# Other rows for the mixing steps beside units 1 and 2, and another order of unit 0's decay, products and doubling, in a two-layer streaming encoder

## The chip, the cores and the metric

The kernel runs on one core of a Trainium2 chip, as one launch. The metric is the device time in microseconds (us), lower being better. A core has five engines that run their own instruction streams in order and meet at semaphores: PE (TensorE, matrix products into the accumulators, called banks), DVE (VectorE), ACT (ScalarE), POOL (GpSimd) and SP (SyncE). Sixteen DMA engines move the data; here SP's queue issues the loads of weights, and POOL's queue the gathers of table rows.

## What is computed

The reference is a trunk of two layers over 256 tokens of 1024 numbers. Each layer normalises, projects once (`h @ w_in`), and gives the columns to three branches whose outputs are joined and projected back; then a retrieval step picks 128 experts of 16384 for each token.

```
for l in range(2):
    h = rms_norm(x, norm_mix[l]);  cols = h @ w_in[l]
    y_a = diff_attention(cols_a, ...)       # 4 heads, softmax(0) - lam * softmax(1), block-causal in chunks of 64
    y_b = s5_mixer(cols_b, ...)             # 1024 complex states, diagonal scan over the tokens, then a gated unit
    y_c = rwkv7_mixer(cols_c, ...)          # 4 heads, S = S*w + (S @ -kk) b^T + v k^T, y = S r, for every token
    x = x + concat(y_a, y_b, y_c) @ w_out[l]
    x = x + peer_ffn(rms_norm(x, norm_ffn[l]), ...)

# peer_ffn for a block of 128 tokens
s = einsum(q, sub_keys); top 16 of each half; best 16 of the 256 sums, for each of 8 heads
act = gelu(einsum('thkd,td->thk', u_tab[expert], h))
out = einsum('thk,thkd->td', softmax(best) * act, v_tab[expert])
```

## The kernel before

The 256 tokens are two tiles of 128, and with two layers this makes four units, n = 0 to 3: layer n // 2, tile n % 2. A unit has a mixing part (projection, three branches, output projection), then a part that chooses experts, and then 256 table rows: for each of 128 slots one row of u and one of v, each 1024 numbers for 128 tokens (512 KB). POOL gathers them (line 618) into a ring of 16 buffers (`arena`). DVE multiplies a u row with the token and sums (lines 1833 and 1835). A v row is scaled and added up by PE, as two 128x512 products with a diagonal matrix that ACT makes (lines 2430, 2431, 1057), or in one case of three from slot 32 on by DVE (lines 1842 and 1846). A buffer is gathered anew once its user has let go of it.

The mixing and the choosing of unit n + 1 are cut into named steps, which stand between the rows of unit n. `ROWS_BY[n]` gives for each step the row before which it stands, 0 to 256, and DVE, PE and ACT all read the same table: `by_rows` and `gather` put the rows and the steps into each engine's stream. So the order is written out in full; nothing is scheduled at run time. Table 0 belongs to unit 0's rows and unit 1's steps, table 1 to unit 1's rows and unit 2's steps, table 2 to unit 2's rows and unit 3's steps. Unit 0's own steps have no rows to stand between; its order is in the functions `first`, one for each engine.

The steps, in their order: bc0 to bc4 and da0 to da5 are chunks of the projection, one load of weights (1 MB) and 3.6 us of PE or less each, through a ring of three buffers (`wring`) that SP fills again when a chunk has been multiplied. At da0 and da2 DVE turns the inputs of the state-space branch (`s5_turn`), at da3 and da4 it scans them (8 scans each), at da5, rot and sd it turns back and adds; gelu, glu, tanh, glud, gss are its gated unit. abkr is `products`, which makes the inputs al, bm, km, rp of the delta rule; mats are their products on PE (lines 2092); at masked DVE masks them and starts the inverse of a triangular 128x128 matrix per head. The inverse takes six levels k: p is the product on PE (lines 2117, 2122), c its copy on ACT (line 840) and the next level's factor on DVE (line 1238), u the update on PE (lines 2132, 2134), d its copy on ACT (lines 847, 848). The attention hangs on some of them: scores and their maxima at level 1 and 3, the softmax on ACT after levels 2 and 4, DVE's `combined` (line 1334) at d2 and d4. rhs, rhsd, sa, y, mean and so on end the delta rule, out3 and xm the mixing, fT to id4 choose the experts.

In unit 0 DVE also computes the turning factors of the state-space branch by doubling (`phase_doubling`, k from 0 to 6); the last and largest is k = 6.

Of the kernel before, what the change touches and what calls it, by code (L numbers as in the profile page):

```python
# [18 lines left out]
ALU = mybir.AluOpType  # L19
# [68 lines left out]
for _s in range(SLOTS - LEAD):  # L88
# [24 lines left out]
        "tanh": 100, "glud": 103, "gss": 104, "abkr": 108, "mats": 108, "masked": 119, "p1": 123, "c1": 125,  # L113
# [3 lines left out]
        "yd": 172, "mean": 175, "dev": 180, "var": 181, "vara": 185, "outd": 196, "out3": 196, "xm": 196, "fsq":  # L117
# [9 lines left out]
        86, "glu": 89, "tanh": 92, "glud": 92, "gss": 102, "abkr": 102, "mats": 102, "masked": 111, "p1": 116,  # L127
# [3 lines left out]
        "y": 165, "yd": 169, "mean": 169, "dev": 170, "var": 170, "vara": 170, "outd": 170, "out3": 173, "xm":  # L131
# [72 lines left out]
def build_program(nc, A, out):  # L204
    ctx = ExitStack()
    with ctx:
# [418 lines left out]
        def _(act):  # L625
# [53 lines left out]
            def mixing(n, layer, t):  # L679
# [191 lines left out]
                def first():  # L871
# [20 lines left out]
                    kk_length()  # L892
                    own(A_(small_a[:, 30:31], eps[:, 0:1], ACT.Exp))
                    decays()
                    output_map()
                    squares()
                    input_map()
                    qk_lengths()
# [1573 lines left out]
```

## Time and profile before

| | |
|---|---|
| median of three runs | 1729.08 us (1728.06 to 1729.99) |
| the profiled execution: its time, its span | 1729.59 us, 1727.8 us |
| mean granted TensorE clock, of full speed | 0.924 |
| PE busy, share of the span | 1339.9 us, 78% |
| DVE | 1390.0 us, 80% |
| POOL | 1137.9 us, 66% |
| ACT | 406.1 us, 24% |
| DMA | 640.89 MB, mean 371 GB/s; gathers 538.25 MB |

The span goes from the first to the last instruction. Busy shares are means over stages with different limits; an engine that isn't the limit of a stage costs nothing by idling there. A wait is put down to what released it last. The DMA share is a relative measure: where the queues are never empty it reads 1.03.

### The profile page before, as it was taken

How to read it: one execution, taken by the hardware profiler on the slowest of the kernel's cores; microseconds unless marked ns; L12 is line 12 of the kernel's file. 1: busy time of each engine (PE TensorE's matmuls, PEld its weight loads, DVE VectorE, ACT ScalarE, POOL GpSimd, SP SyncE). 2: the span in 40 equal slices, each digit the busy share in tenths (PEclk: the TensorE clock that was granted, in tenths of full speed). 3: DMA queues.
4: the chain of work that ended last, by engine and by line, in shares of the span. 5: the costliest groups of instructions: out<-in, count | busy, mean ns of one | idle time of the engine just before them, and what ended most of it. 6: DMA issues, size and time to landing. Idle time of an engine off the chain costs nothing. (4 is left out here: it accounts for less than half of the span.)

```text
span 1727.8 us, 17677 instructions
## 1 busy us (share of the span) xinstructions
PE 1339.9 (78%) x5322; PEld 755.4 (44%) x5322; DVE 1390.0 (80%) x3383; ACT 406.1 (24%) x977; POOL 1137.9 (66%) x1046
## 2 busy tenths in 40 slices
PE   6989689688889397867887868978888837765667
PEld 6568444255456163444454453444545412222222
DVE  7867999996779789996777898987777897687663
ACT  2442312333211221413221122313221121101000
POOL 2002776777775876477767777577777777777773
PEclk9999899999999699999999979989999969988889
DMA  7348999999999999899999999999999999999997
GB/s 236 135 158 284 398 403 362 410 382 365 408 402 399 404 393 405 313 357 355 385 393 404 403 404 407 366 375 354 387 403 402 409 410 409 410 409 410 409 409 313
DMA packets 204721, 640.89 MB, mean 371 GB/s; under 512 B 18602, under 2 KB 35860, under 8 KB 204628
## 3 DMA queue, kind: packets, MB, share of 16 engines
q0 software_dynamic: 147920, 538.25, 80.0%
q1 hardware_dynamic: 56172, 100.96, 16.2%
q8 instruction: 43, 0.70, 0.2%
q10 hardware_dynamic: 536, 0.57, 0.1%
q14 instruction: 50, 0.41, 0.1%
HBM read 638.65 MB, written 1.05 MB: 370 GB/s over the span
## 5 line engine op out<-in xcount | busy, mean ns | idle before, releaser
L618 POOL DMA_INDIRECT arena<-in_peer_u_dram,expert x512 | 562.0, 1098 | 346.1 <-issue 139.7
L618 POOL DMA_INDIRECT arena<-in_peer_v_dram,expert x512 | 566.3, 1106 | 210.2 <-issue 139.3
L2430 PE MATMUL bank<-arena,diag 128*128 128x512 f32 x768 | 433.8, 648 | 242.4 <-DMA arena<-in_peer_v_dram,expert 171.1
L1835 DVE SCALAR_TENSOR_TENSOR arena<-arena,normed 128x1024 f32<-128x1024 f32 x364 | 434.5, 1225 | 63.0 <-DMA arena<-in_peer_u_dram,expert 58.6
L2431 PE MATMUL bank<-arena,diag 128*128 128x512 f32 x768 | 416.9, 626 | 0.0
L2430 PEld LDWEIGHTS bank<-arena,diag 128*128 128x128 f32 x768 | 133.8, 199 | 453.7 <-issue 386.9
L2431 PEld LDWEIGHTS bank<-arena,diag 128*128 128x128 f32 x768 | 154.3, 201 | 200.3 <-issue 200.3
L1833 DVE SCALAR_TENSOR_TENSOR arena<-arena,bank 128x1024 f32<-128x1024 f32 x148 | 176.9, 1219 | 80.7 <-DMA arena<-in_peer_u_dram,expert 80.1
L1057 ACT ACTIVATE diag<-ident,weight 128x128 f32<-128x128 f32 x384 | 129.9, 392 | 211.5 <-DVE weight L1852 119.6
L1910 PE MATMUL bank<-h_cm,wring 128*128 128x128 f32 x1152 | 143.6, 287 | 27.8 <-DMA wring<-in_peer_w_q_dram 8.4
L1910 PEld LDWEIGHTS bank<-h_cm,wring 128*128 128x128 f32 x1152 | 141.3, 202 | 39.6 <-issue 24.5
L1846 DVE SCALAR_TENSOR_TENSOR x<-arena,weight,x 128x1024 f32<-128x1024 f32 x96 | 123.5, 1286 | 21.8 <-DMA arena<-in_peer_v_dram,expert 20.2
L1926 PE MATMUL bank<-wring,h_cm 128*128 128x512 f32 x192 | 91.6, 626 | 10.6 <-DMA wring<-in_w_in_dram 8.7
L1061 ACT ACTIVATE dots<-dots 128x16 f32<-128x16 f32 x32 | 6.9, 216 | 332.7 <-DVE arena L1835 174.6
L1926 PEld LDWEIGHTS bank<-wring,h_cm 128*128 128x128 f32 x192 | 37.5, 201 | 57.4 <-issue 41.8
L1934 PE MATMUL bank<-wring,h_cm 128*128 128x512 f32 x128 | 59.7, 613 | 2.2 <-DVE h_cm L1562 1.1
L1842 DVE SCALAR_TENSOR_TENSOR bank<-arena,weight,bank 128x1024 f32<-128x1024 f32 x30 | 38.6, 1288 | 14.2 <-DMA arena<-in_peer_v_dram,expert 13.3
L1061 ACT ACT_TABLE_LOAD x24 | 30.8, 1283 | 61.7 <-DVE arena L1835 33.1
L1791 DVE SCALAR_TENSOR_TENSOR work<-work 128x64 f32<-128x64 f32 (+1 forms) x320 | 41.1, 202 | 0.7
L1934 PEld LDWEIGHTS bank<-wring,h_cm 128*128 128x128 f32 x128 | 25.1, 199 | 31.9 <-issue 29.5
L840 ACT ACTIVATE work<-bank 128x512 f32<-128x512 f32 x24 | 14.2, 593 | 83.6 <-PE bank L2122 83.3
L2122 PEld LDWEIGHTS bank<-work 128*128 128x128 f32 x192 | 24.9, 191 | 14.4 <-issue 10.4
(445 smaller groups left out, 1534.7 us busy)
## 6 DMA issues: line engine op xcount, KB each, us to landing
wring<-in_w_in_dram SPq DMA_DIRECT2D x40, 1024.0 KB, 12.9
wring<-in_peer_w_q_dram SPq DMA_DIRECT2D x25, 1024.0 KB, 15.0
wring<-in_w_out_dram SPq DMA_DIRECT2D x16, 1024.0 KB, 8.9
arena<-in_peer_u_dram,expert POOLq DMA_INDIRECT x512, 12.8
arena<-in_peer_v_dram,expert POOLq DMA_INDIRECT x512, 13.7
arena<-in_peer_w_q_dram SPq DMA_DIRECT2D x7, 1024.0 KB, 11.5
wring<-in_w_in_dram SPq DMA_DIRECT2D x4, 512.0 KB, 13.2
x<-in_x_dram SPq DMA_DIRECT2D x2, 512.0 KB, 5.3
```

What stands on the lines that cost most here:

```text
L618: nc.gpsimd.indirect_dma_start(out=rows[g % RING], out_offset=None, in_=tables[kind], in_offset=bass.IndirectOffsetOnAxis(ap=expert[:, n % ...
L1057: A_(diag[:, p % DIAGS, :], ident[:, :], ACT.Copy, scale=weight[:, slot:slot + 1]).then_inc(s_diag, 1)
L1791: last = stt(picks[c // 8][:, c % 8, :].rearrange("p (a b) -> p a b", b=TOPK), places, float(c), ids, ALU.is_equal, ALU.mult)
L1833: ins = stt(row2, row2, 1.0, hb_psum[n], ALU.mult, ALU.mult, accum_out=dots[:, slot:slot + 1])
L1835: ins = stt(row, row, 1.0, hb, ALU.mult, ALU.mult, accum_out=dots[:, slot:slot + 1])
L1842: ins = stt(total, row2, weight[:, slot:slot + 1], so_far, ALU.mult, ALU.add)
L1846: ins = stt(x[:, t, :], row, weight[:, slot:slot + 1], x[:, t, :], ALU.mult, ALU.add)
L1910: last = mm(bank[b0 + j][:, 0:P], w[:, k, P * j:P * j + P], source[:, 4 * part + k, :], start=part == 0 and k == 0, stop=part == 1 and k == 3)
L1926: last = mm(bank[b0][:, :], h_cm[:, 4 * part + k, :], w[:, k, :], start=part == 0 and k == 0, stop=part == 1 and k == 3)
L1934: last = mm(bank[4 + half_][:, :], mixed[:, OUT_K[name] + k, :], w[:, k, 512 * half_:512 * half_ + 512], start=name == "out0" and k == 0, ...
L2430: mm(bank[6][:, :], d, row[:, 0:512], start=first, stop=end)
L2431: mm(bank[7][:, :], d, row[:, 512:1024], start=first, stop=end).then_inc(s_pe_used, 1)
```

## The change

Three things are changed. First, table 1 (rows of unit 1, steps of unit 2) from exp4 on to d6, and second, table 2 (rows of unit 2, steps of unit 3) from late_id4 to masked, give their steps other rows. The values of table 0 and table 3 stay. Of table 1, row before and row now:

| step | late_id4 | gate4 | da0 | da1 | da2 | da3 | da4 | da5 | rot | sy | sd | glu | glud | abkr | mats |
|---|---|---|---|---|---|---|---|---|---|---|---|---|---|---|---|
| before | 65 | 71 | 71 | 71 | 71 | 73 | 74 | 75 | 75 | 77 | 83 | 89 | 92 | 102 | 102 |
| now | 65 | 65 | 66 | 69 | 72 | 76 | 80 | 85 | 89 | 92 | 96 | 101 | 106 | 111 | 113 |

| step | masked | p1, c1 | u1, d1 | p2 | c2 | u2, d2 | p3 | c3 | u3, d3 | p4, c4 | u4, d4 | p5 | c5 | p6 to u6 | d6 | rhs |
|---|---|---|---|---|---|---|---|---|---|---|---|---|---|---|---|---|
| before | 111 | 116 | 118 | 124 | 126 | 126 | 136 | 136 | 139 | 144 | 144 | 147 | 149 | 153 | 154 | 156 |
| now | 121 | 124 | 127 | 131 | 132 | 133 | 138 | 139 | 141 | 145 | 146 | 149 | 150 | 154 | 155 | 156 |

Of table 2:

| step | late_id4 | da0 | da1 | da2 | da3 | da4 | da5 | rot | sy | glud | gss | abkr | mats | masked |
|---|---|---|---|---|---|---|---|---|---|---|---|---|---|---|
| before | 46 | 48 | 53 | 54 | 54 | 54 | 56 | 65 | 68 | 91 | 91 | 91 | 91 | 97 |
| now | 45 | 46 | 49 | 52 | 56 | 60 | 64 | 66 | 69 | 84 | 85 | 87 | 89 | 98 |

Third, in unit 0 the last doubling moves behind level 3 of the inverse, the sum of squares behind the start of the inverse; PE does the inner products ahead of chunk da3 and waits for bm by a semaphore of its own, and ACT copies the input map ahead of the squares.

```diff
@@ ROWS_BY, table 1 (one line of it) @@
-        "da0": 71, "da1": 71, "da2": 71, "da3": 73, "da4": 74, "da5": 75, "rot": 75, "sy": 77, "sd": 83, "gelu":
+        65, "da0": 66, "da1": 69, "da2": 72, "da3": 76, "da4": 80, "da5": 85, "rot": 89, "sy": 92, "sd": 96,
@@ ACT, first() @@
                     output_map()
+                    input_map()
                     squares()
-                    input_map()
                     qk_lengths()
@@ DVE, products() @@
-                    own.add(tt(rw["bm"][:, :, :], rw["bm"][:, :, :], rw["em"][:, :, :], ALU.mult))
+                    bm = tt(rw["bm"][:, :, :], rw["bm"][:, :, :], rw["em"][:, :, :], ALU.mult)
+                    if n == 0:
+                        bm.then_inc(ab_ok, 1)
+                    else:
+                        own.add(bm)
@@ DVE, first() @@
                     setup_input()
-                    phase_doubling(0, 6)
                     decay()
                     products()
+                    inverse_begun()
                     qk_sums()
-                    inverse_begun()
                     rest_masked()
                     next_level(2)
                     qk_normed()
                     next_level(3)
+                    phase_doubling(0, 6)
                     s5_turn(0)
@@ PE, first() @@
                     pe.wait_ge(kk_sd, 1)
+                    bd_turns()
                     to_rows(0, "da2", qkb[1])
-                    bd_turns()
+                    pe.wait_ge(ab_ok, 1)
+                    pe.wait_ge(st_done, 1)
+                    inner_products()
                     to_rows(0, "da3", qkb[1])
                     pe.wait_ge(abkr, 1)
-                    pe.wait_ge(st_done, 1)
-                    inner_products()
                     pe.wait_ge(st_input, 1)
-                    pe.wait_ge(lora_ok, 1)
-                    pe.wait_ge(kk_sd, 1)
                     outer_products()
```

The instructions of three places, before and after (the line numbers after are 1 to 5 higher). The first is DVE in unit 0: before, the last doubling (lines 1219 to 1227) stands between the input map and the decay (lines 1352 to 1358).

```order
L1197 COPY small_p<-ident 128x1
L1219 TENSOR_TENSOR normed<-e_cos 128x512
L1220 TENSOR_TENSOR e_cos<-e_sin 128x8x64
L1222 TENSOR_TENSOR e_cos<-normed,e_cos 128x8x64
L1224 TENSOR_TENSOR normed<-e_cos,e_sin 128x512
L1225 TENSOR_TENSOR e_sin<-e_sin,e_cos 128x8x64
L1227 TENSOR_TENSOR e_sin<-normed,e_sin 128x8x64
L1352 TENSOR_SCALAR rw_a<-rw_a 128x256
L1353 TENSOR_SCALAR rw_ep<-rw_ep 128x256
L1355 SCALAR_TENSOR_TENSOR cum<-ones,rw_ep 128x128 x2
L1358 TENSOR_SCALAR small_m<-cum 128x2
```

After, the decay follows at once, and the doubling (lines 1220 to 1228) stands behind the factor of level 3 (line 1239) and ahead of the first turn (line 1247).

```order
L1198 COPY small_p<-ident 128x1
L1353 TENSOR_SCALAR rw_a<-rw_a 128x256
L1354 TENSOR_SCALAR rw_ep<-rw_ep 128x256
L1356 SCALAR_TENSOR_TENSOR cum<-ones,rw_ep 128x128 x2
L1359 TENSOR_SCALAR small_m<-cum 128x2
```

And the later place, also after:

```order
L1239 TENSOR_TENSOR work<-work,level 128x512
L1220 TENSOR_TENSOR normed<-e_cos 128x512
L1221 TENSOR_TENSOR e_cos<-e_sin 128x8x64
L1223 TENSOR_TENSOR e_cos<-normed,e_cos 128x8x64
L1225 TENSOR_TENSOR normed<-e_cos,e_sin 128x512
L1226 TENSOR_TENSOR e_sin<-e_sin,e_cos 128x8x64
L1228 TENSOR_TENSOR e_sin<-normed,e_sin 128x8x64
L1247 TENSOR_TENSOR arena<-bank,e_cos 128x512
L1248 TENSOR_TENSOR arena<-bank,e_sin 128x512
```

So six instructions moved from ahead of the decay to ahead of the first turn. The second place is PE in unit 0, before: three chunks of four products (`x12`), the turns of the input map (line 2075), the fourth chunk, then the inner products (al with bm, bm with al) and the outer ones.

```order
L1926 MATMUL bank<-wring,h_cm 128x512 x12
L2075 MATMUL bank<-ident,arena 128x128 x8
L1926 MATMUL bank<-wring,h_cm 128x512 x4
L2092 MATMUL bank<-rw_al,rw_bm 128x128 x4
L2092 MATMUL bank<-rw_bm,rw_al 128x128 x4
L2092 MATMUL bank<-rw_al,rw_km 128x128 x4
L2092 MATMUL bank<-rw_rp,rw_bm 128x128 x4
L2092 MATMUL bank<-rw_rp,rw_km 128x128 x4
L2117 MATMUL bank<-ident 128x512
```

After, the turns stand behind the second chunk and the inner products ahead of the fourth.

```order
L1931 MATMUL bank<-wring,h_cm 128x512 x8
L2080 MATMUL bank<-ident,arena 128x128 x8
L1931 MATMUL bank<-wring,h_cm 128x512 x4
L2097 MATMUL bank<-rw_al,rw_bm 128x128 x4
L2097 MATMUL bank<-rw_bm,rw_al 128x128 x4
L1931 MATMUL bank<-wring,h_cm 128x512 x4
L2097 MATMUL bank<-rw_al,rw_km 128x128 x4
L2097 MATMUL bank<-rw_rp,rw_bm 128x128 x4
L2097 MATMUL bank<-rw_rp,rw_km 128x128 x4
L2122 MATMUL bank<-ident 128x512
```

So the inner products moved ahead of a chunk. The third place is DVE beside the rows of unit 1, steps da3 to rot of unit 2, before: 16 scans (line 1262) stand in one piece, with one row product (line 1835) ahead of the turning back (lines 1267 to 1270) and none ahead of the decay.

```order
L1835 SCALAR_TENSOR_TENSOR arena,dots<-arena,normed 128x1024
L1444 TENSOR_SCALAR rw_lora<-rw_lora 64x128
L1447 TENSOR_SCALAR rw_kk<-cc,pcol 128x128 x2
L1450 TENSOR_TENSOR rw_k<-rw_kk 128x256
L1262 SCALAR_TENSOR_TENSOR work<-mag,work 128x128 x16
L1835 SCALAR_TENSOR_TENSOR arena,dots<-arena,normed 128x1024
L1267 TENSOR_TENSOR work<-e_cos,work 128x1024
L1268 TENSOR_TENSOR work<-e_sin,work 128x1024
L1270 TENSOR_TENSOR work<-work 128x1024
L1352 TENSOR_SCALAR rw_a<-rw_a 128x256
L1353 TENSOR_SCALAR rw_ep<-rw_ep 128x256
```

After, the scans are two pieces of 8 with row products (lines 1840, 1851) between them, ahead of them and behind them.

```order
L1840 SCALAR_TENSOR_TENSOR arena,dots<-arena,normed 128x1024 x2
L1449 TENSOR_SCALAR rw_lora<-rw_lora 64x128
L1452 TENSOR_SCALAR rw_kk<-cc,pcol 128x128 x2
L1455 TENSOR_TENSOR rw_k<-rw_kk 128x256
L1263 SCALAR_TENSOR_TENSOR work<-mag,work 128x128 x8
L1840 SCALAR_TENSOR_TENSOR arena,dots<-arena,normed 128x1024 x2
L1857 TENSOR_TENSOR weight<-gate,dots 128x16
L1263 SCALAR_TENSOR_TENSOR work<-mag,work 128x128 x8
L1840 SCALAR_TENSOR_TENSOR arena,dots<-arena,normed 128x1024 x3
L1268 TENSOR_TENSOR work<-e_cos,work 128x1024
L1269 TENSOR_TENSOR work<-e_sin,work 128x1024
L1271 TENSOR_TENSOR work<-work 128x1024
```

So the same steps stand among more rows.

## Rows read from the trace of the kernel before

**Rows 1.** Waits of POOL: engine, line, releaser; us in total, times, longest.

```profile
POOL arena L618 <- DVE expert L1797: 139.6, 1, 139.6
```

**Rows 2.** Stretches: us, busy by engine, clock, DMA share, GB/s.

```profile
671.00:720.00 49.00, 40.32 (x137) 18.00 (x135) 47.28 (x116) 10.46 (x26) 23.28 (x22) 0.97 0.92 351
720.00:827.00 107.00, 80.86 (x350) 46.80 (x344) 88.88 (x170) 38.06 (x90) 85.35 (x72) 0.95 0.95 350
1049.00:1130.00 81.00, 71.85 (x220) 32.36 (x219) 78.31 (x197) 22.48 (x59) 50.36 (x43) 0.98 1.00 381
1130.00:1240.00 110.00, 86.52 (x372) 50.83 (x371) 86.36 (x159) 30.09 (x70) 86.94 (x76) 0.94 0.98 370
1460.00:1700.00 240.00, 153.70 (x272) 53.43 (x270) 168.31 (x328) 28.26 (x79) 178.11 (x188) 0.89 1.03 409
```

**Rows 3.** Timeline of DVE, unit 1: start, us, instruction, idle and releaser.

```profile
671.36 1.23 DVE L1835 SCALAR_TENSOR_TENSOR arena<-arena,normed 128x1024 f32<-128x1024 f32 x1 [1.32 <-DMA arena<-in_peer_u_dram,expert]
...
785.51 0.18 DVE L1334 RECIPROCAL small_a<-small_a 128x4 f32<-128x4 f32 x1 [5.41 <-ACT wring L768]
...
833.90 0.49 DVE L1523 COPY work<-bank 128x128 f32<-128x128 f32 x2 [3.46 <-PE bank L2147]
...
909.85 1.22 DVE L1835 SCALAR_TENSOR_TENSOR arena<-arena,normed 128x1024 f32<-128x1024 f32 x1 [0.33 <-DMA arena<-in_peer_u_dram,expert]
```

**Rows 4.** Waits of DVE from 690 to 865 us.

```profile
DVE small_a L1334 <- ACT wring L768: 13.6, 2, 8.2
...
DVE work L1523 <- PE bank L2147: 3.5, 1, 3.5
DVE bank L1320 <- PE bank L1993: 2.6, 1, 2.6
```

**Rows 5.** Timeline of POOL, unit 1.

```profile
719.39 1.85 POOL L618 DMA_INDIRECT arena<-in_peer_v_dram,expert  x1 [10.89 <-PE bank L2431]
...
725.88 1.97 POOL L618 DMA_INDIRECT arena<-in_peer_v_dram,expert  x1 [0.30 <-PE bank L2431]
...
814.56 0.94 POOL L618 DMA_INDIRECT arena<-in_peer_v_dram,expert  x1 [0.30 <-issue]
```

**Rows 6.** Timeline of DVE, one row product of unit 1.

```profile
725.83 1.21 DVE L1835 SCALAR_TENSOR_TENSOR arena<-arena,normed 128x1024 f32<-128x1024 f32 x1
```

**Rows 7.** Waits of DVE from 1090 to 1265 us.

```profile
DVE arena L1835 <- DMA arena<-in_peer_u_dram,expert: 8.6, 6, 1.9
```

**Rows 8.** Timeline of DVE, unit 2.

```profile
1136.44 1.23 DVE L1835 SCALAR_TENSOR_TENSOR arena<-arena,normed 128x1024 f32<-128x1024 f32 x1 [1.94 <-DMA arena<-in_peer_u_dram,expert]
...
1237.06 1.23 DVE L1835 SCALAR_TENSOR_TENSOR arena<-arena,normed 128x1024 f32<-128x1024 f32 x1 [1.23 <-DMA arena<-in_peer_u_dram,expert]
```

**Rows 9.** Timeline of POOL, unit 2.

```profile
1098.65 1.68 POOL L618 DMA_INDIRECT arena<-in_peer_u_dram,expert  x1 [8.98 <-DVE arena L1835]
```

**Rows 10.** Timeline of DVE, unit 0.

```profile
45.66 0.69 DVE L1219 TENSOR_TENSOR normed<-e_cos 128x512 f32<-128x512 f32 x1
...
55.41 0.42 DVE L1372 TENSOR_TENSOR rw_bm<-rw_bm,rw_em 128x256 f32<-128x256 f32 x1
...
61.37 1.22 DVE L1456 TENSOR_REDUCE small_m<-arena 128x16 f32<-128x1024 f32 x1 [2.18 <-ACT arena L705]
...
65.40 0.69 DVE L1496 TENSOR_TENSOR work<-work,ident 128x512 f32<-128x512 f32 x1
```

**Rows 11.** Timeline of PE, unit 0.

```profile
56.98 3.60 PE L1926 MATMUL bank<-wring,h_cm 128*128 128x512 f32 x8
60.51 0.72 PE L2092 MATMUL bank<-rw_al,rw_bm 64*128 64x128 f32 x8
...
66.15 1.12 PE L2117 MATMUL bank<-ident 128*128 128x512 f32 x2 [2.00 <-DVE work L1496]
...
106.65 1.13 PE L2134 MATMUL bank<-work 128*128 128x128 f32 x8 [0.84 <-ACT work L840]
```

**Rows 12.** Timeline of ACT, unit 0.

```profile
51.34 0.20 ACT L689 ACTIVATE small<-small 128x4 f32<-128x4 f32 x1 [2.41 <-DVE small_m L1358]
```

More of the change, by code:

```diff
@@ L108 @@
         "scale": 14, "exp1": 14, "gate1": 14, "turn": 14, "turned": 17, "bc0": 17, "late_t2a": 20, "late_t2b":
[4 rows of a table removed]
-        "tanh": 100, "glud": 103, "gss": 104, "abkr": 108, "mats": 108, "masked": 119, "p1": 123, "c1": 125,
[3 rows of a table removed]
-        "yd": 172, "mean": 175, "dev": 180, "var": 181, "vara": 185, "outd": 196, "out3": 196, "xm": 196, "fsq":
[4 rows of a table removed]
[4 rows of a table added]
+        "glu": 97, "tanh": 100, "glud": 103, "gss": 104, "abkr": 108, "mats": 108, "masked": 119, "p1": 123,
[3 rows of a table added]
+        "saa": 167, "y": 170, "yd": 172, "mean": 175, "dev": 180, "var": 181, "vara": 185, "outd": 196,
[4 rows of a table added]
     {
@@ L124 @@
         "late_t3b": 35, "late_t3c": 35, "bc1": 38, "late_id3": 38, "bc2": 38, "exp3": 38, "gate3": 45, "bc3":
[2 rows of a table removed]
-        86, "glu": 89, "tanh": 92, "glud": 92, "gss": 102, "abkr": 102, "mats": 102, "masked": 111, "p1": 116,
[3 rows of a table removed]
-        "y": 165, "yd": 169, "mean": 169, "dev": 170, "var": 170, "vara": 170, "outd": 170, "out3": 173, "xm":
[4 rows of a table removed]
[2 rows of a table added]
+        "gelu": 98, "glu": 101, "tanh": 103, "glud": 106, "gss": 108, "abkr": 111, "mats": 113, "masked": 121,
[3 rows of a table added]
+        "sa": 164, "saa": 164, "y": 165, "yd": 169, "mean": 169, "dev": 170, "var": 170, "vara": 170, "outd":
[4 rows of a table added]
     {
         "exp0": 0, "square": 0, "gate0": 0, "late_t3a": 0, "scale": 0, "turn": 0, "turned": 2, "bc0": 8,
[3 rows of a table removed]
-        77, "glu": 78, "tanh": 78, "glud": 91, "gss": 91, "abkr": 91, "mats": 91, "masked": 97, "p1": 101, "c1":
[3 rows of a table removed]
-        157, "yd": 157, "mean": 160, "dev": 160, "var": 160, "vara": 160, "outd": 165, "out3": 165, "xm": 169,
[4 rows of a table removed]
[3 rows of a table added]
+        "gelu": 77, "glu": 78, "tanh": 78, "glud": 84, "gss": 85, "abkr": 87, "mats": 89, "masked": 98, "p1":
[3 rows of a table added]
+        156, "saa": 156, "y": 157, "yd": 157, "mean": 160, "dev": 160, "var": 160, "vara": 160, "outd": 165,
[4 rows of a table added]
     {
         "exp0": 6, "gate0": 15, "late_t3a": 44, "late_t3b": 44, "late_t3c": 52, "late_id3": 60, "exp3": 69,
-        "gate3": 80, "late_t4a": 92, "late_t4b": 93, "late_t4c": 113, "late_id4": 133, "exp4": 145, "gate4": 156},
+        "gate3": 80, "late_t4a": 92, "late_t4b": 93, "late_t4c": 113, "late_id4": 133, "exp4": 145, "gate4":
+        156},
 )
@@ L406, in build_program @@
         kk_sq, kk_sd, cum_ok, exps = sem("kk_sq"), sem("kk_sd"), sem("cum_ok"), sem("exps")
-        abkr, mats, mats_out, masked, all_masked, tr_ps, tok_ok = sem("abkr"), sem("mats"), sem("mats_out"), sem("masked"), sem("all_masked"), sem("tr_ps"), sem("tok_ok")
+        ab_ok, abkr, mats, mats_out, masked, all_masked, tr_ps, tok_ok = sem("ab_ok"), sem("abkr"), sem("mats"), sem("mats_out"), sem("masked"), sem("all_masked"), sem("tr_ps"), sem("tok_ok")
         ms_ok, pr_ps, pr_ok, up_ps, inv_ok, invT_ok = (sem(i) for i in ("ms_ok", "pr_ps", "pr_ok", "up_ps", "inv_ok", "invT_ok"))
```

58 rows, old and new, of the table ROWS_BY are left out of this document.

## The prediction

> **What bounds the kernel now.** I read four views: the windows (busy time, DMA share), the waits of POOL, the timeline of DVE where it waited, and the timelines of the first 66 us. Three regimes show.
>
> First the head. POOL's first gather waits 139.6 us for the expert numbers of unit 0 [rows 1], and until then no table row can be fetched, so every microsecond by which the chain of unit 0 is shorter comes off the end, one for one.
>
> Second, stretches in which the 16 DMA engines are full. Their share reads 1.03 and they move 409 GB/s; 188 gathers in 240 us are 1.28 us for one of 512 KB [rows 2]. There nothing but bytes counts, and this change has the same bytes.
>
> Third, the mixing steps between the rows of units 1 and 2, where the share falls to 0.92 and 0.95 in unit 1 and to 1.00 and 0.98 in unit 2 [rows 2]. Against 1.03 that is 0.11 x 49 + 0.08 x 107 = 14 us of idle DMA in unit 1 and 0.03 x 81 + 0.05 x 110 = 7.9 us in unit 2. At most this can be won there. What ends the waits differs, and this decides my numbers:
>
> In unit 1 DVE waits for a gathered row at 671.36 us and then not again until 909.85 [rows 3]. In between it works (47.28 of 49 us, 88.88 of 107 [rows 2]) or waits for PE and ACT: 13.6 us for the softmax, 2.6 for the scores, 3.5 for the right side [rows 4]. No DMA stands in that list. The gathers come too late for nobody; POOL's wait of 10.89 us at 719.39 [rows 5] is a sign that the ring of 16 rows is full, not a cost of its own.
>
> In unit 2 it is otherwise: DVE waits six times for a gathered row, 8.6 us in all [rows 7], the most of them around 1136 and around 1237 us [rows 8], after POOL had stood 8.98 us at 1098.65 on a full ring [rows 9].
>
> **Part 1, unit 0.** Before, DVE does the last doubling from 45.66 us, six instructions and 4.1 us, ahead of the decay [rows 10]. ACT sat idle 2.41 us for that decay [rows 12]. Without the doubling the decay is 4.1 us earlier, but ACT must first load its table, so the exponentials, and rw_bm after them, come 2.4 us earlier: 55.83 becomes 53.4 [rows 10]. PE does a chunk of four 128x512 products in 3.60 us [rows 11]. Before, three chunks, the turns (1.04), a fourth chunk and then the inner products at 60.51 us; now the fourth chunk stands behind them, so they start 3.5 us earlier, at 57.0, with rw_bm long there. DVE masks from 58.2 instead of 62.6 us, since the sum of squares (1.22 us, and 2.18 of waiting for the fourth chunk's squares [rows 10]) stands behind the masks now. The end of the masks moves from 66.1 to about 62.0 us. PE still has the fourth chunk and the outer products ahead of level 1: 57.0 + 1.1 + 3.6 + 1.6 = 63.3 (the first eight products took from 60.51 to 61.6, the twelve outer ones then some 1.6), instead of 66.15 [rows 11]. So 2.8 us at level 1. The doubling is paid later, ahead of the first turn of the state-space part: DVE is 3 us ahead there and takes on 4.1, so the turned k and with it the scores come 1 us later than before, and PE, which is 2.8 us ahead, waits 0.3 to 0.5 us for them. I take 2.4 us for the head. Bounds: 0 (the doubling costs all where PE waits for k) and 3.5 (all that PE gains). What hides the doubling is PE's lead of 2.8 us; with that cover gone it costs up to 4.1 us.
>
> **Part 2, unit 1.** The same instructions on every engine, over other rows. Rows 71 to 75 held five chunks and all of the state-space steps; now they lie on rows 66 to 89. The levels p1 to d6 had rows 116 to 154 and now have 124 to 155, because the masks moved from row 111 to 121. DVE's work to row 155 is unchanged, and DVE had no wait for rows to lose. What can shrink are its waits for PE and ACT. (a) combined(1): product, copy, update, copy and softmax of level 4 all hung on row 144, now on 145 and 146, so up to one row of work (1.2 us) covers the start of it. (b) combined(0): 0.6 us, the copy of level 2 being one row ahead of its update. (c) PE finds rows landed that it had to wait for, as the ring is fuller; I take 1.6 us. (d) Against it, level 6 ends one row later while the right side stays at row 156: 1.4 us more in the wait that is 3.5 now. Sum 2.0 us won. Bounds: the 13.6 + 2.6 us of waits all gone, and 8.2 us lost (the third rival). I stay near the low end because the trace's own waits, not POOL's stall, end last there.
>
> **Part 3, unit 2.** The chunks and scans that stood at rows 53 to 56 go to rows 49 to 64, and the gated part, the products and the matrices of unit 3 from row 91 to 84, 87 and 89. With 16 scans no longer in one piece, DVE lets go of its row about 7 us sooner, and POOL's 8.98 us shrink. The five weight loads of 1 MB go through SP's queue in the same stretch and still need the same DMA time, so the next rows land only 2 to 4 us sooner; after that POOL keeps its lead. The six waits (8.6 us) and the idle DMA (7.9 us) bound this from two sides, nearly alike. I take 7.0 us. Bounds 0 and 8.6, plus the few us that PE's waits could give.
>
> What stands in a wait's way: PE is in order, so rows of unit 1 and 2 queue behind a chunk that waits for its weights; before this was so with four chunks in a row, now with one.
>
> **Sum.** 2.4 + 2.0 + 7.0 = 11.4 us off the profiled execution's 1729.59 (span 1727.8 and 1.8 around it): 1718.2. The median is 1729.08, 0.5 lower, so 1718 serves for both.
>
> **POOL's pace.** While POOL waits for nothing, it issued 60 gathers from 725.88 to 814.56 us, 1.48 us for one, more than the 1.28 of the full DMA [rows 5]. The gather at 725.88 took 1.97 us, the one at 814.56 0.94; the first began 0.05 us behind a row product of DVE that lasts 1.21 us [rows 5, 6], and 1.21 - 0.05 + 0.94 is 2.1. So row products slow the issue. The Trainium skill ("SBUF — State Buffer", section "SBUF: two separate sides") says that a DVE instruction with two SBUF inputs and a GpSimd operation that reads SBUF exclude each other for the whole instruction. By that rule, the trace agrees. The rule speaks against part 3: the row products stay as many, so POOL's pace in the stretch would stay, and if nothing but the pace counts the 7.0 us fall away and the sum is 2.4 + 2.0 = 4.4 us, or 1725; that is the mechanism of rival B, whose time stands there on its own.
>
> **Rivals.**
> A. The dependency waits of unit 1 are really missing rows in disguise: PE came late to its updates since rows landed late. Then some 12 of the 16.2 us go. For it: PE is busy only 80.86 of 107 us there [rows 2]. Against: it also has level after level to wait for. 1729.6 - 2.4 - 12 - 7 = 1708. Chance 0.18.
> B. POOL's 1.48 us is the limit of unit 2 from row 75 on and it never waits there anyway, so a shorter stall only fills the DMA queues sooner and the waits at 1136 and 1237 stay. Only head and unit 1 count: 1729.6 - 2.4 - 2 = 1725. If unit 1 gives nothing either, 1727. For it: the share of 0.98 without a full ring [rows 2]. Against: a lead at POOL isn't lost before the ring is full again. Chance 0.22.
> C. Slower. The chain of levels through PE and ACT sets the pace, not the rows. It now starts 10 rows later in unit 1 (111 to 121), which is 8.2 us of DVE's row work (two rows in three at 1.23), and it had 48.4 us from 785.51 to 833.90 [rows 3] over 33 rows and gets 26. If it doesn't shrink, row 159 comes 8.2 us later; in unit 2, where PE is busy 71.85 of 81 us [rows 2], the rows' waits return as waits for that chain. 1729.6 + 8.2 - 2.4 = 1735. It decides once the levels cost over 6 us more than their rows. Against: unit 0 runs the six levels with no rows between in 41.6 us, from 66.15 to 107.8 [rows 11], and the 34 rows in question need 50 at POOL's pace. Chance 0.09.
> D. The change does the rows' part but nothing in the head (the doubling eats it): 1720.6, inside my own range. Chance 0.06.
>
> **How the numbers follow.** Forecast 1718 with 0.45, its own range 1713 to 1723; A 0.18, B 0.22, C 0.09, D 0.06. A difference under 0.2% (3.5 us) can't be told from none here. Faster than 1725.6: forecast, A, D and a third of B, 0.77. The rest of B, 0.15, is within; C, but for a hundredth that ends within 3.5 us, is slower, 0.08. For 8 in 10 the range reaches to A's value and past B's: 1708 to 1728.
>
> **What would show it.** In the changed profile POOL's first wait is about 137.2 us instead of 139.6, and the masks end near 62. POOL's waits of over 5 us near 719 and 1098 are gone. DVE waits for gathered rows in 1090 to 1265 add up to under 2 us instead of 8.6. DVE's wait for the right side of unit 1 is near 5 us. Wrong would be: waits for the softmax in unit 1 under 5 us in all (then A), POOL waits gone but DVE's six waits for rows still there (B), or a wait of over 8 us at the right side or the scores (C).

## The result, and the profile after

The changed kernel takes 1717.39 us (median of 6 runs, 1713.52 to 1719.70) against 1729.53 us (6 runs, 1726.30 to 1735.32) of the kernel before: a ratio of 0.992 with an interval of 0.991 to 0.994, or 12 us less by the medians (the ratios in this document compare fast executions only and are not exactly the quotients of the medians). The forecast was 1718. But the profiled execution is the shortest of the six, 1713.52 us with a span of 1711.7, so its rows show 16 us, 4 more than the median. The shares of the parts are therefore taken from several profiled executions, further below. POOL issues one gather for each of a unit's 256 rows, so "gather 64" below is the issue of row 64.

The first wait of POOL, the answer to [rows 1], and the first products of unit 0 on PE, the answer to [rows 11] (timeline: start, us, instruction):

```profile
POOL arena L619 <- DVE expert L1802: 136.0, 1, 136.0
```

```profile
56.61 0.72 PE L2097 MATMUL bank<-rw_al,rw_bm 64*128 64x128 f32 x8
...
63.08 1.12 PE L2122 MATMUL bank<-ident 128*128 128x512 f32 x2
```

And rw_bm and the end of the masks on DVE, to [rows 10]:

```profile
52.71 0.42 DVE L1373 TENSOR_TENSOR rw_bm<-rw_bm,rw_em 128x256 f32<-128x256 f32 x1
...
60.76 0.69 DVE L1501 TENSOR_TENSOR work<-work,ident 128x512 f32<-128x512 f32 x1
```

POOL's wait fell from 139.6 to 136.0 us. The inner products start at 56.61 us instead of 60.51, the masks end at 61.5 instead of 66.1, level 1 starts at 63.08 instead of 66.15.

The stretches of units 1 and 2, to [rows 2] (us, busy time of PE, PE's weight loads, DVE, ACT and POOL with their instructions, clock, DMA share, GB/s):

```profile
667.50:720.00 52.50, 47.75 (x128) 23.12 (x127) 50.95 (x122) 9.77 (x28) 35.66 (x32) 0.97 1.02 400
720.00:820.00 100.00, 76.64 (x361) 46.24 (x360) 86.89 (x166) 39.64 (x89) 76.39 (x66) 0.90 0.96 353
1040.00:1120.00 80.00, 73.27 (x221) 33.89 (x221) 77.96 (x196) 23.97 (x59) 55.73 (x48) 0.95 1.03 406
1120.00:1230.00 110.00, 91.64 (x407) 55.67 (x406) 86.73 (x154) 31.01 (x71) 84.66 (x77) 0.92 0.97 365
```

In the first half of the steps of unit 1 the DMA share rose from 0.92 to 1.02. In the second it is as it was, 0.96. In unit 2 it rose from 1.00 to 1.03 in the first half and fell from 0.98 to 0.97 in the second. The stretches before and after do not hold quite the same rows: the first half of unit 1 holds 22 gathers before and 32 after. Over the same gathers of unit 1, 70 to 186, before and then after:

```profile
671.00:865.00 194.00, 156.87 (x607) 83.89 (x605) 162.78 (x326) 55.51 (x128) 135.49 (x117) 0.96 0.95 358
```

```profile
667.50:853.90 186.40, 156.03 (x607) 86.29 (x605) 163.09 (x326) 56.23 (x129) 135.29 (x117) 0.94 0.98 374
```

DVE, PE and POOL are busy for the same time in both, to 1 us. What went, 7.6 us, is waiting.

POOL's longest wait from 700 to 830 us, and in unit 2, to [rows 5, 9]:

```profile
712.75 1.85 POOL L619 DMA_INDIRECT arena<-in_peer_v_dram,expert  x1 [3.00 <-PE bank L2435]
```

```profile
1067.20 1.49 POOL L619 DMA_INDIRECT arena<-in_peer_u_dram,expert  x1 [5.32 <-DVE arena L1840]
```

The waits of 10.89 and 8.98 us are gone; the longest left there are 3.00 and 5.32. The waits of DVE in the stretch that was 671 to 865 us, to [rows 4], and from 1090 to 1265 us, to [rows 7]:

```profile
DVE small_a L1335 <- ACT wring L769: 10.4, 2, 6.4
DVE rw_ep L1560 <- ACT rw_ep L869: 3.1, 1, 3.1
...
DVE work L1528 <- PE bank L2152: 2.3, 1, 2.3
...
DVE bank L1321 <- PE bank L1998: 0.6, 1, 0.6
```

```profile
DVE bank L1321 <- PE bank L1998: 6.4, 1, 6.4
DVE arena L1840 <- DMA arena<-in_peer_u_dram,expert: 6.1, 3, 2.8
```

The softmax costs DVE 10.4 us instead of 13.6, the right side 2.3 instead of 3.5, the scores 0.6 instead of 2.6. In unit 2 the waits for gathered rows are 6.1 us instead of 8.6.

What the forecast had not read is the list of PE's waits. Before, from 671 to 865 us, and after, from 667.5 to 853.5:

```profile
PE bank L2430 <- DMA arena<-in_peer_v_dram,expert: 11.9, 9, 3.5
```

```profile
PE bank L2097 <- DVE small_m L1396: 6.1, 1, 6.1
...
PE bank L2434 <- DMA arena<-in_peer_v_dram,expert: 0.6, 1, 0.6
```

Before, PE waited nine times, 11.9 us in all, for a v row that had not landed, the longest from 788 to 791 us. After, one such wait of 0.6 us is left in the stretch. In unit 2 it is less of a change: from 1049 to 1240 us before, PE waits 14.9 us for v rows, from 1040 to 1230 after, 9.8.

### The profile page after: what moved, and what is told of

It reads as the page before. It is cut to its first block and busy times, and to the rows that moved or that the text cites. A ratio compares the mean times of both kernels' runs of the same rounds, so it can differ in the third digit from the quotient of the medians.

```text
span 1711.7 us, 17672 instructions
## 1 busy us (share of the span) xinstructions
PE 1342.8 (78%) x5322; PEld 762.1 (45%) x5322; DVE 1390.7 (81%) x3383; ACT 407.2 (24%) x977; POOL 1135.1 (66%) x1046
## 3 DMA queue, kind: packets, MB, share of 16 engines
q1 hardware_dynamic: 56172, 100.96, 16.4%
## 5 line engine op out<-in xcount | busy, mean ns | idle before, releaser
L619 POOL DMA_INDIRECT arena<-in_peer_v_dram,expert x512 | 560.6, 1095 | 201.4 <-issue 136.0
L1838 DVE SCALAR_TENSOR_TENSOR arena<-arena,bank 128x1024 f32<-128x1024 f32 x148 | 176.9, 1219 | 80.3 <-DMA arena<-in_peer_u_dram,expert 79.6
L1915 PEld LDWEIGHTS bank<-h_cm,wring 128*128 128x128 f32 x1152 | 143.9, 206 | 40.2 <-issue 25.3
L1931 PE MATMUL bank<-wring,h_cm 128*128 128x512 f32 x192 | 87.8, 603 | 0.3 <-DMA wring<-in_w_in_dram 0.3
L1939 PE MATMUL bank<-wring,h_cm 128*128 128x512 f32 x128 | 58.0, 599 | 1.9 <-DVE h_cm L1567 1.1
L1023 ACT ACTIVATE work<-bank 128x512 f32<-128x512 f32 (+1 forms) x20 | 10.1, 506 | 89.0 <-PE bank L1915 76.5
## 6 DMA issues: line engine op xcount, KB each, us to landing
arena<-in_peer_w_q_dram SPq DMA_DIRECT2D x7, 1024.0 KB, 11.5
```

Of the source, the lines that this page charges most:

```text
L619: nc.gpsimd.indirect_dma_start(out=rows[g % RING], out_offset=None, in_=tables[kind], in_offset=bass.IndirectOffsetOnAxis(ap=expert[:, n % ...
L1838: ins = stt(row2, row2, 1.0, hb_psum[n], ALU.mult, ALU.mult, accum_out=dots[:, slot:slot + 1])
L1915: last = mm(bank[b0 + j][:, 0:P], w[:, k, P * j:P * j + P], source[:, 4 * part + k, :], start=part == 0 and k == 0, stop=part == 1 and k == 3)
L1931: last = mm(bank[b0][:, :], h_cm[:, 4 * part + k, :], w[:, k, :], start=part == 0 and k == 0, stop=part == 1 and k == 3)
L1939: last = mm(bank[4 + half_][:, :], mixed[:, OUT_K[name] + k, :], w[:, k, 512 * half_:512 * half_ + 512], start=name == "out0" and k == 0, ...
```

## Experiments

The first eight kernels ran on two other chips, on which the kernel before takes 1823.50 and 1839.94 us. There the gathers move less in the last unit, as a window of the first experiment shows beside 1.03 and 409 of [rows 2]:

```profile
1460.00:1700.00 240.00, 138.97 (x261) 50.61 (x260) 169.65 (x394) 34.23 (x95) 164.59 (x172) 0.86 0.97 376
```

The windows hold different rows, but the same gathers say the same: gathers 65 to 251 of unit 3 take 1.28 us each in the kernel before of [rows 2] and 1.40 to 1.44 in four kernels on these chips. The single executions of the kernel before lie 1.6% and 2.2% apart, so the parts are also read from the times at which POOL starts its gathers. The last four ran on a chip on which the kernel before takes 1729.40 us (9 runs, 1727.70 to 1733.79), like the first.

**Unit 0 alone.** All tables as before.

```diff
 ROWS_BY: all four tables as before
+DVE, PE, ACT first(): the order of the changed kernel
```

> The kernel before with the new order of unit 0 alone (all four tables as before). Theory P, the terms as forecast: the head is worth 2.4 us, so 1726.6 to 1727.1 beside 1729. Theory Q, the terms as the changed kernel's rows read: POOL's first wait fell from 139.6 to 136.0 us and the whole 3.6 us stays until the end, 1725.5. Theory R, the head is given back: the rows after it run into the full ring or the full DMA of unit 0, under 1 us is left at the end.

Measured: 1821.87 us, ratio 0.998 (0.994 to 1.002); POOL's first gather starts at 156.3 us. The time is too coarse to tell P from Q or from nothing. The start is not: in seven kernels with the new order of unit 0 (one of them with the doubling back) it lies at 156.1 to 157.0 us, in the seven with the old one at 158.8 to 161.2. Theory R is neither shown nor excluded by this run; the table further below bears on it.

**Table 1 alone.**

```diff
-ROWS_BY[1]: as before
+ROWS_BY[1]: as in the changed kernel
```

> The kernel before with table 1 of the changed kernel alone. P, as forecast: 2.0 us less, 1727. Q, as the rows read: 7.8 us less between row 64 of unit 1 and its end, 1721, with POOL's 10.9 us wait at 719 gone, and the gain already there at row 80 of unit 1. R: most of the gain of unit 1 depended on the earlier start, under 1 us without it.

Measured: 1810.20 us, ratio 0.992 (0.990 to 0.995). That is 14 us (9 to 19), seven times the forecast's 2.0, and needs neither the head nor table 2. P and R fall, and Q's 7.8 us, right in its direction, is below this interval too. POOL issues rows 64 to 96 of unit 1 in 47.8 us, against 63.9 and 62.4 in the two kernels on this chip with table 1 as before; at row 80 nothing is gained yet (25.5 us from row 64 against 26.0 and 25.9), other than Q had it.

**Table 2 alone.**

```diff
-ROWS_BY[2]: as before
+ROWS_BY[2]: as in the changed kernel
```

> The kernel before with table 2 of the changed kernel alone. P, as forecast: 7.0 us less, 1722. Q, as the rows of the changed kernel read: 4.5 us less (that execution was the shortest of six, so 1 to 4.5), 1724.5 to 1728. Rival B: POOL's pace limits unit 2 and the waits of DVE for rows stay, under 1 us less.

Measured: 1815.39 us, ratio 0.9945 (0.991 to 0.998), or 4 to 16 us: P and the upper end of Q are left, B is not, on this chip. Run again on another chip, below, the table does not exclude B.

**The first half of table 1.**

```diff
-"late_id4": 65, "exp4": 66, "gate4": 71, "da0": 71, "da1": 71, "da2": 71, "da3": 73, "da4": 74, "da5": 75, "rot": 75, "sy": 77,
+"late_id4": 65, "exp4": 65, "gate4": 65, "da0": 66, "da1": 69, "da2": 72, "da3": 76, "da4": 80, "da5": 85, "rot": 86, "sy": 87,
-"sd": 83, "gelu": 86, "glu": 89, "tanh": 92, "glud": 92, "gss": 102,
+"sd": 89, "gelu": 91, "glu": 93, "tanh": 94, "glud": 96, "gss": 102,
```

> The kernel before with only the first half of table 1 changed: chunks and state-space steps spread over rows 66 to 85 as in the changed kernel, the rest of the state-space steps at 86 to 96, products, matrices, masks and levels at the rows of before. Theory E: unit 1's gain comes from the DVE piece that no longer stands still on a full ring (POOL's 10.9 us wait), so nearly all of the 7.8 us are here, 1721 to 1723. Theory L: it comes from the levels and the waits for PE and ACT, which don't move here, so 0 to 2 us, 1727 to 1729.

Measured: 1816.64 us, ratio 0.997 (0.993 to 1.001). The interval reaches from nothing to 12 us and excludes neither E nor L. What it makes of POOL's waits is shown with its counterpart below.

**The changed kernel again, and each of the two tables alone again**, on the second of these chips.

> The changed kernel once more, as the yardstick for the parts that run on the same chip. On a chip like the first (1729 before): 1716 to 1718, ratio 0.992. On a chip like that of the first four experiments (1823 before, where gathers land unevenly): the parts there gave 0.998, 0.992 and 0.9945, which would add up to 0.985, and less than that if the parts overlap.

> The kernel before with table 1 of the changed kernel alone, a second time. P, as forecast: 2.0 us less. Q, as the rows of the changed kernel read: 7.8 us less, a ratio of 0.9955, gained between row 64 and row 96 of unit 1.

> The kernel before with table 2 of the changed kernel alone, a second time. P, as forecast: 7.0 us less, a ratio of 0.996. Q: 1 to 4.5 us less, a ratio of 0.9975 to 0.9995.

Measured: 1816.47 us, ratio 0.986 (0.980 to 0.991), for all; 1828.46, ratio 0.992 (0.988 to 0.995), for table 1; 1830.85, ratio 0.9985 (0.994 to 1.003), for table 2. Table 1 gives the same twice, above Q's 7.8 us both times (9 to 19 and 9 to 22). Table 2 gave 0.9945 and 0.9985 (the quotient of the medians is 0.995 for the second as well), and its own time stays unclear. The whole is worth 1.4% there and 0.8% on the first chip.

**The second half of table 1.**

```diff
-"masked": 111, "p1": 116, "u1": 118, "p2": 124, "u2": 126, "p3": 136, "u3": 139, "p4": 144, "u4": 144, "p5": 147, "p6": 153, "d6": 154,
+"masked": 121, "p1": 124, "u1": 127, "p2": 131, "u2": 133, "p3": 138, "u3": 141, "p4": 145, "u4": 146, "p5": 149, "p6": 154, "d6": 155,
```

> The kernel before with only the second half of table 1 changed: chunks, state-space steps, products and matrices at the rows of before (up to row 102), masks and levels at the rows of the changed kernel (121 to 155). Theory E (the gain of unit 1 is made by spreading the first half): 0 to 1 us, since POOL's 10.9 us wait at 719 stays. Theory L (it is made by the levels and the waits for PE and ACT): 5 us or more. Rival C of the forecast: slower, up to 8 us, by waits at the softmax and the right side.

Measured: 1842.95 us, ratio 1.000 (0.996 to 1.004). Rival C is not seen, though up to 7 us slower is inside the interval, and theory L falls: the levels at their new rows give nothing by themselves. POOL's longest waits from gather 50 to 100 of unit 1 in it, and then in the kernel with the first half alone:

```profile
687.58 1.68 POOL L619 DMA_INDIRECT arena<-in_peer_u_dram,expert  x1 [9.05 <-DVE arena L1836]
...
756.28 0.94 POOL L619 DMA_INDIRECT arena<-in_peer_v_dram,expert  x1 [11.17 <-PE bank L2432]
...
767.16 1.47 POOL L619 DMA_INDIRECT arena<-in_peer_v_dram,expert  x1 [8.71 <-PE bank L2432]
```

```profile
668.16 1.68 POOL L619 DMA_INDIRECT arena<-in_peer_u_dram,expert  x1 [5.98 <-DVE arena L1836]
...
742.19 1.19 POOL L619 DMA_INDIRECT arena<-in_peer_v_dram,expert  x1 [4.79 <-PE bank L2432]
```

With the levels moved alone, waits of 9.05, 11.17 and 8.71 us stand; with the first half moved the longest are 5.98 and 4.79. From gather 64 of unit 1 to the first of unit 2, POOL takes on the one chip 327.1 and 327.0 us with the table as before, 324.0 with the first half new and 318.3 with the whole; on the other 332.2 as before, 330.3 with the second half new, and 312.6 and 317.3 with the whole. So the first half gives 3 of 9 us, the second alone 2 of 17, and only the two together the whole. A possible reason, not tested: with the masks at row 121 the steps ahead of them can have rows 85 to 113.

The kernel with the first half alone also shows what late v rows cost by themselves. In it PE waits for no v row at all between gathers 70 and 187 of unit 1 (698 to 893 us); in the two kernels on this chip with the table as before it waits 6.7 and 5.0 us there. DVE's waits in the same stretch add up to 29.5 us, against 37.9 and 29.9 in those two and 26.2 with the whole of table 1, where PE still waits 3.8 us for a v row. So taking the late v rows away is not enough for the gain.

**Table 0 evenly as well**, on top of the changed kernel (gelu to mats, not shown, move by 1 to 3 rows too).

```diff
-"late_t4a": 54, "late_t4b": 54, "late_t4c": 54, "late_id4": 54, "exp4": 58, "gate4": 58,
+"late_t4a": 52, "late_t4b": 54, "late_t4c": 56, "late_id4": 57, "exp4": 59, "gate4": 60,
-"da0": 68, "da1": 68, "da2": 69, "da3": 76, "da4": 76, "da5": 82, "rot": 83, "sy": 84, "sd": 96,
+"da0": 62, "da1": 64, "da2": 67, "da3": 71, "da4": 75, "da5": 79, "rot": 83, "sy": 85, "sd": 91,
```

> The changed kernel with table 0 (rows of unit 0, steps of unit 1) set evenly as well: late_t4a to gate4 on rows 52 to 60 instead of 54 to 58, da0 to da5 on 62, 64, 67, 71, 75, 79 instead of 68, 68, 69, 76, 76, 82. Before and after, POOL stands 8.9 us on a full ring at 261.95 us (row 70 of unit 0) and PE then waits for gathered v rows. Theory Q (a stall of POOL turns into late v rows, and through PE into DVE's waits at the inverse and the softmax): unit 0 gives 4 to 8 us more, POOL's time from gather 64 to 192 of unit 0 falls by as much. Theory P (a full ring costs nobody anything where DVE waits for no row): 0 to 1 us.

Measured: 1718.77 us, ratio 0.994 (0.993 to 0.996), no better than the changed kernel; from gather 64 to 192 of unit 0 POOL takes 199.0 us against 198.7. The gather that waited 8.93 us in the changed kernel, number 70 of unit 0 (in the kernel before it waited 10.17, at 265.74), and the same one at 255.30 here:

```profile
261.95 1.68 POOL L619 DMA_INDIRECT arena<-in_peer_u_dram,expert  x1 [8.93 <-DVE arena L1840]
```

```profile
255.30 0.94 POOL L619 DMA_INDIRECT arena<-in_peer_u_dram,expert  x1 [0.30 <-issue]
```

The stall is gone, and gather 70 starts 6.7 us sooner. The windows of the changed kernel and of this one:

```profile
240.00:280.00 40.00, 34.10 (x81) 14.41 (x82) 38.93 (x124) 8.11 (x23) 24.66 (x23) 0.91 0.97 361
...
320.00:360.00 40.00, 25.69 (x101) 14.94 (x102) 38.97 (x80) 9.53 (x18) 31.77 (x28) 0.83 1.03 409
```

```profile
240.00:280.00 40.00, 35.51 (x86) 15.48 (x85) 38.87 (x124) 8.22 (x23) 25.47 (x25) 0.91 1.03 405
...
320.00:360.00 40.00, 25.99 (x99) 15.96 (x100) 39.01 (x78) 6.89 (x14) 31.78 (x28) 0.79 1.00 377
```

The DMA share rose from 0.97 to 1.03 from 240 to 280 us, and fell from 1.03 to 1.00 from 320 to 360. By gather 96 the lead is gone (302.0 us against 301.9). So here P was right and Q wrong. PE's waits for v rows between 245 and 446 us did fall, from 9.8 to 5.2 us, and DVE's for the softmax from 11.3 to 10.1, and the stretch is no shorter. What the DMA moved more before 280 us it moves less after 320, where POOL's own pace leaves no room in either kernel (31.8 us busy and 28 x 0.30 us of issue, 40.2 of 40).

**The scans in one piece again**, in the changed kernel.

```diff
 DVE, beside_rows()
                     yield "da3"
                     lora_inputs()
-                    s5_scan(0)
                     yield "da4"
+                    s5_scan(0)
                     s5_scan(1)
```

> The changed kernel, but DVE's 16 scans in units 1 to 3 in one piece again, at da4 (row 80 and row 60), with PE's chunks left where they are. Theory D (DVE's long piece holds the ring, as the forecast's part on unit 2 had it): POOL's issue of rows 64 to 112 of unit 1 and 64 to 96 of unit 2 becomes 3 to 7 us slower for each. Theory PE (chunks in a pile on PE hold back the v rows, and with them the ring): under 1 us each.

Measured: 1716.30 us, ratio 0.993 (0.991 to 0.994), the changed kernel's own. The 16 scans stand in one piece:

```profile
703.06 5.34 DVE L1263 TENSOR_TENSOR_SCAN work<-mag,work 128x128 f32<-128x128 f32 x16
```

POOL's issue of rows 64 to 112 of unit 1 takes 80.3 us against 79.6 in the changed kernel (90.8 before), of rows 64 to 96 of unit 2 53.3 against 53.3 (60.7 before). Theory D falls, for chunks that are spread over the rows.

**PE's later chunks in one pile**, in the changed kernel.

```diff
 PE, steps of a unit
                 yield "da3"
-                to_rows(n, "da3", qkb[0])
                 yield "da4"
-                (waits), lora()
-                to_rows(n, "da4", qkb[1])
                 yield "da5"
+                to_rows(n, "da3", qkb[0])
+                (waits), lora()
+                to_rows(n, "da4", qkb[1])
                 to_rows(n, "da5", qkb[1])
```

> The changed kernel, but PE does the chunks da3 and da4 of units 1 to 3 only at da5's place (row 85 and row 64), so that three chunks stand in one pile, with DVE's steps left where they are. Theory PE: no v row can be done in 11 us and more, POOL stands still for as long as the ring doesn't cover, and the issue of rows 64 to 112 of unit 1 and 64 to 96 of unit 2 becomes 3 to 8 us slower for each. Theory D: under 1 us each.

Measured: 1717.68 us, ratio 0.993 (0.9915 to 0.994). The pile is there, and lasts from 708.4 to 721.0 us:

```profile
708.44 3.60 PE L1931 MATMUL bank<-wring,h_cm 128*128 128x512 f32 x8
...
714.17 7.03 PE L1931 MATMUL bank<-wring,h_cm 128*128 128x512 f32 x16
721.03 1.02 PE L2434 MATMUL bank<-arena,diag 128*128 128x512 f32 x2
```

Rows 64 to 112 take 78.6 us, less than the changed kernel's 79.6, and rows 64 to 96 of unit 2 again 53.3. Theory PE, as it stood there, falls too: a pile of three chunks costs nothing where the scans are spread. The scans in one piece and the chunks in a pile together, as the kernel before has them, were not run. What the kernel before had is also longer. PE's timeline in it, from the first da chunk on:

```profile
681.46 7.03 PE L1926 MATMUL bank<-wring,h_cm 128*128 128x512 f32 x16
690.37 3.70 PE L1926 MATMUL bank<-wring,h_cm 128*128 128x512 f32 x8 [1.88 <-DVE work L1253]
693.91 1.02 PE L2430 MATMUL bank<-arena,diag 128*128 128x512 f32 x2
...
697.25 3.70 PE L1926 MATMUL bank<-wring,h_cm 128*128 128x512 f32 x8 [1.46 <-DMA wring<-in_w_in_dram]
700.78 1.02 PE L2430 MATMUL bank<-arena,diag 128*128 128x512 f32 x2
...
704.80 3.68 PE L1926 MATMUL bank<-wring,h_cm 128*128 128x512 f32 x8
712.00 5.40 PE L1926 MATMUL bank<-wring,h_cm 128*128 128x512 f32 x8 [3.52 <-DMA wring<-in_w_in_dram]
717.24 1.02 PE L2430 MATMUL bank<-arena,diag 128*128 128x512 f32 x2
```

and in the changed kernel:

```profile
683.88 3.60 PE L1931 MATMUL bank<-wring,h_cm 128*128 128x512 f32 x8
687.31 1.02 PE L2434 MATMUL bank<-arena,diag 128*128 128x512 f32 x2
...
689.03 1.02 PE L2434 MATMUL bank<-arena,diag 128*128 128x512 f32 x2
...
690.74 3.60 PE L1931 MATMUL bank<-wring,h_cm 128*128 128x512 f32 x8
```

Before, six chunks lie from 681.5 to 717.2 us with v rows at 693.91 and 700.78 only: two in 36 us, with two waits for the weights among them (1.46 and 3.52 us). The ring's 16 rows of 1.28 us [rows 2] cover 20 us. In the changed kernel one or two v rows stand behind every chunk, and in the pile a hole of 13 us without a v row costs nothing. But no single hole of the kernel before is longer than 15 us either (679 to 693.9, and 702.6 to 717.2). So it is not one long hole that fills the ring there; two holes with two v rows between them may, and this is an estimate from the rows, since no such pair of holes was run alone.

**The last doubling back ahead of the decay**, in the changed kernel.

```diff
 DVE, first()
                     setup_input()
+                    phase_doubling(0, 6)
                     decay()
...
                     next_level(3)
-                    phase_doubling(0, 6)
```

> The changed kernel with the last doubling of unit 0 ahead of the decay again (4.1 us of DVE), the rest of the new order kept. Read by POOL's first wait: 136.0 us in the changed kernel, 139.6 before. Theory H1 (the move of the doubling carries the gain of the head, the inner products then wait for bm): 138 us or more. Theory H2 (the place of the inner products ahead of a chunk carries it, and the doubling was hidden): 136.0 to 136.8.

Measured: 1718.68 us, ratio 0.994 (0.992 to 0.9955). POOL's first wait, and PE:

```profile
POOL arena L619 <- DVE expert L1802: 136.6, 1, 136.6
```

```profile
58.47 0.72 PE L2097 MATMUL bank<-rw_al,rw_bm 64*128 64x128 f32 x8 [0.43 <-ACT small_a L677]
...
64.91 1.13 PE L2122 MATMUL bank<-ident 128*128 128x512 f32 x2
```

Level 1 starts 1.8 us later than in the changed kernel, but the first wait is 136.6 us, inside what four executions with the new order of unit 0 show here and on the first chip (136.0 to 136.9). H1 falls: the doubling was hidden. H2's number holds, but not that the inner products alone carry the gain: level 1 is only 1.2 us earlier here than in the kernel before (64.91 against 66.15) and the first wait is 3.0 us shorter. The turns, the sum of squares and ACT's input map also stand elsewhere, and they were not taken apart.

## Why the prediction was right in its sum and wrong in its parts

The time came out within 1 us. Its terms did not: unit 1 gave 5.1 us more than forecast and unit 2 4.3 us less. That these made up for each other is luck. How much sooner than in the kernel before (one profiled execution of 1729.59 us) the five kernels on chips of its kind start their gathers, in us:

| | first gather | unit 1, gather 64 | unit 2, first | unit 3, first | last |
|---|---|---|---|---|---|
| changed | 3.6 | 3.6 | 11.3 | 15.6 | 16.4 |
| table 0 too | 2.6 | 3.0 | 10.3 | 12.7 | 12.3 |
| scans in one | 3.2 | 1.2 | 8.1 | 10.1 | 11.5 |
| chunks in a pile | 2.9 | 1.4 | 8.3 | 11.2 | 11.3 |
| doubling back | 3.0 | 1.5 | 8.2 | 9.9 | 10.5 |
| mean | 3.1 | 2.1 | 9.2 | 11.9 | 12.4 |

All columns are taken against that one execution, and executions of the kernel before lie up to 9 us apart, so the five rows agree better with each other than the split is certain.

**Head, forecast 2.4.** Measured 3.1 at the first gather. At the first gather of unit 1 only 0.5 us of it are there in the mean (2.1, 1.7, -0.5, 0.0 and -0.7 in the order of the table), at gather 64 of unit 1 again 2.1. So the forecast's "one for one" until the end is not shown, and the 2.4 us cannot be told from a smaller gain. The steps held: inner products at 57.0 forecast and 56.6 measured, masks ended 62.0 and 61.5, level 1 63.3 and 63.1. What was wrong is that the doubling's place was to matter; with it moved back the first gather comes 0.6 us later, inside the scatter.

**Unit 1, forecast 2.0.** Measured 7.1, from 6.7 to 7.7 in each of the five. The term was mis-sized, and one of its parts had the wrong sign. DVE's waits over the same gathers fell by 3.2 us (softmax; forecast 1.8 in (a) and (b)), 2.0 (scores; forecast nothing), 1.2 (right side; forecast 1.4 more in (d)), 0.9 (square root) and 0.6, together 7.9 us. Part (c), late v rows at PE, was priced at 1.6 us without PE's waits having been read; they were 11.9 us and fell to 0.6.

The premise behind the small term was that POOL's wait of 10.89 us was "not a cost of its own", since DVE waited for no row. DVE did not, but PE did, inside the product and update chain that DVE's softmax and scores hang on. That this is how the stall was paid for is likely and not shown. For it speaks that both kinds of wait fell together. Against it speak two runs: with the first half of table 1 alone PE waited for no v row, and only 3 of 9 us came; with table 0 even, PE's waits for v rows fell by 4.6 us and nothing came. That the levels' new rows alone are not the cause, the experiment with the second half shows. What is shown is that it takes both halves of table 1; which wait carries the gain stays open. So whether rival A was right in kind is open too; at 12 us it was too large, since 10.4 us of softmax stay.

**Unit 2, forecast 7.0.** Measured 2.7, from 1.7 to 4.3, on chips like the first. The step that failed is "after that POOL keeps its lead", with all 7.9 us of idle DMA taken as won. POOL gains 7.4 us between rows 64 and 96, alike in all eight executions with the new table (53.3 us against 60.7), but the DMA had been idle only 0.03 x 81 = 2.4 us of that stretch, by the forecast's own sum. Of the 13.0 to 17.7 us that the gathers are ahead at row 96, 9.9 to 15.6 are left at unit 3's first. The rest of the lead at POOL is, as I read it, a longer DMA queue. The other 5.5 us of idle DMA lay from 1130 to 1240, and the share there is 0.97 now instead of 0.98. That half is rival B's: POOL issues 77 gathers in 110 us, 84.66 us busy and 0.30 us of issue before each, together 107.8 of 110, so its own pace takes nearly all of the time, before (86.94 + 76 x 0.30 = 109.7 of 110 [rows 2]) and after. DVE's waits for rows fell from 8.6 to 6.1 us, not under 2. The scans, which were to carry the gain, carry none where the chunks are spread, and the pile of chunks none where the scans are; what shortens rows 64 to 96 by 7.4 us stays open. B's time, 1725, missed mostly because unit 1 gave 7 us. Whether DVE's row products make POOL's pace was not tried.

The count of idle DMA fits unit 1 as well: over the same gathers it fell from 0.08 x 194 = 15.5 us to 0.05 x 186.4 = 9.3, or 6.2 of the 7.1 us.

Rival C is not seen. Rival D, a head that gives nothing, is not seen at the first gather; what is left of the head at the end is not shown.

Open also is why the whole change is worth 23 us on the chip of 1840 us and 12 on those of 1729. POOL takes 410.8 to 416.3 us from the first gather of unit 2 to that of unit 3 with table 2 new and 423.5 to 429.8 without, some 13 us there, against 3 on the others. A lead in the ring that covers gathers landing unevenly would fit, but nothing tests it.

No kernel beat the changed one beyond the scatter (1716.30 to 1718.77 us).

## What to carry to other kernels

Read the waits of every consumer of a ring, not only of the busiest: DVE waited for no row in unit 1 while PE waited 11.9 us. But do not take such a wait for time that can be won: in unit 0 it fell by 4.6 us and nothing came of it. The length of a stall says little about what its end gives: ends of stalls of 10.9, 9.0 and 8.9 us went with 7, 3 and 0 us. The idle DMA of the stalled stretch, 5.4, 2.4 and 0.06 x 40 = 2.4 us, puts unit 1 first, but it is neither a bound (7 is more than 5.4) nor does it tell the last two apart; the idle DMA of all the steps of a unit, 14 and 7.9 us, did bound the gains of units 1 and 2. Steps need not be set evenly: 16 scans in one piece, or a hole of 13 us between v rows, cost nothing each beside a ring that covers 20 us. And a forecast whose sum is right is to be read part by part: here two misses of 4 to 5 us cancelled.

## What the hardware showed

The same kernel took 1729 us in two series and 1823 and 1840 on two other chips, with a DMA share of 0.97 and 376 GB/s in the last unit where the first have 1.03 and 409, and a mean granted clock near 0.89 where the first have 0.92; why is open. There its executions lie 1.6 and 2.2% apart, against 0.5 and 0.4%. Parts of a few us had to be read there from the starts of the gathers. These agree well in some stretches and not in others: rows 64 to 96 of unit 2 took 53.3 us in all eight executions with the new table 2, and 59.3 to 62.7 in the six with the old one.
